# One chain for the rotation angles, and the index work of the first layer set behind later weight units

## The reference, cut to what matters

```
inv = ROPE_THETA ** (-arange(0, 64, 2) / 64)
ang = positions[..., None] * inv                    # 256 x 32
cos, sin = cos(ang), sin(ang)                       # tables of all rotations
for l in range(2):
    proj = rmsnorm(x, norm_mix[l]) @ w_in[l]        # 1024 -> 5956 columns
    aq, ak, av, iq, ik, iw, hq, hf, hi, hg, ga, gb = split(proj)
    aq = rope(rmsnorm(aq)); ak = rope(rmsnorm(ak))  # 8 heads of 64
    iq = rope(iq); ik = rope(ik)                    # 4 index heads, one key
    score = sum_h iw[h] * relu(iq[h] @ ik.T)        # 256 x 256, causal
    keep the 64 best keys of each query; softmax attention of q, k, v over them
    lb = cumsum(softmax(hgrn_lower_bound))[l] - ... # forget gate's lower bound
    ...                                             # recurrence, gates, output, SwiGLU
```

## Time and profile before

| | |
|---|---|
| median of 3 runs | 1150.14 us (1149.94 to 1151.73) |
| the profiled execution | 1151.75 us, span 1149.7 us |
| PE busy | 1113.0 us, 97% |
| DVE busy | 861.6 us, 75% |
| ACT busy | 622.6 us, 54% |
| `w_lo` on DVE (L1583) | 178 instructions, 401.3 us |
| `w_hi` on ACT (L1054) | 178 instructions, 336.3 us |
| mean DMA rate | 187 GB/s |

### The profile page before, as it was taken

The page is one execution under the profiler, slowest core; times in us unless marked ns, Lnnn a source line. Parts: engine busy times, 40 slices in busy tenths (PEclk is TensorE's granted clock), DMA queues, the critical chain, the costliest instruction groups (busy, mean ns, idle before and its releaser), DMA issues.

```text
span 1149.7 us, 20164 instructions
## 1 busy us (share of the span) xinstructions
PE 1113.0 (97%) x8452; PEld 1065.2 (93%) x8452; DVE 861.6 (75%) x1357; ACT 622.6 (54%) x780; POOL 0.2 (0%) x4
## 2 busy tenths in 40 slices
PE   5999999999999999999999999999999988999997
PEld 5899999999999998999999999999998868999997
DVE  7997766777988877986767788898699966545444
ACT  7677465554444356584664644344588576334333
POOL 0000000000000000000000000000000000000000
PEclk9999999999999999999999999999999998999999
DMA  9646444747879554564346568796555154555520
GB/s 345 210 147 186 145 147 144 254 153 261 278 249 318 164 169 149 156 199 157 122 135 227 193 224 280 245 316 209 160 148 176 43 185 147 184 184 183 184 74 37
DMA packets 176394, 215.14 MB, mean 187 GB/s; under 512 B 5808, under 2 KB 157744, under 8 KB 176304
## 3 DMA queue, kind: packets, MB, share of 16 engines
q1 hardware_dynamic: 175616, 213.20, 56.8%
q10 hardware_dynamic: 688, 0.66, 0.2%
HBM read 212.79 MB, written 1.06 MB: 186 GB/s over the span
## 4 chain that ended last, share of the span: by engine, by line
PE 76%; DVE 17%; ACT 5%; issue 2%; DMA 1%; DVEq 0%; ACTq 0%
PE stream L552 16%; PE stream L554 16%; PE stream L553 16%; DVE w_lo L1583 6%; PE steps L552 6%; PE steps L553 6%; PE steps L554 6%; ACT w_hi L1054 2%; PE stream L636 1%; PE stream L638 1%; PE stream L637 1%; DVE conv_acc L2166 1%; PE steps L966 1%; PE stream L804 1%; DVE conv_acc L2180 1%
## 5 line engine op out<-in xcount | busy, mean ns | idle before, releaser
L1583 DVE TENSOR_TENSOR w_lo<-raw,w_hi 128x2048 fp32r<-128x2048 f32 (+2 forms) x178 | 401.3, 2265 | 175.4 <-ACT w_hi L1054 174.4
L1054 ACT ACTIVATE w_hi<-raw 128x2048 fp32r<-128x2048 f32 (+2 forms) x178 | 336.3, 1893 | 285.3 <-PE stream L554 247.7
L552 PE MATMUL stream<-h_hi,w_hi 128*128 128x256 f32 x1592 | 455.3, 286 | 3.3 <-DVE w_lo L1583 3.0
L553 PE MATMUL stream<-h_lo,w_hi 128*128 128x256 f32 x1592 | 450.4, 283 | 0.0
L554 PE MATMUL stream<-h_hi,w_lo 128*128 128x256 f32 x1592 | 450.4, 283 | 0.0
L552 PEld LDWEIGHTS stream<-h_hi,w_hi 128*128 128x128 f32 x1592 | 305.2, 192 | 7.8 <-DVE w_lo L1583 5.1
L553 PEld LDWEIGHTS stream<-h_lo,w_hi 128*128 128x128 f32 x1592 | 305.4, 192 | 1.4 <-issue 1.0
L554 PEld LDWEIGHTS stream<-h_hi,w_lo 128*128 128x128 f32 x1592 | 305.3, 192 | 0.0
L552 PE MATMUL steps<-gu_hi,w_hi 128*128 128x256 f32 x352 | 99.9, 284 | 0.2 <-DVE gu_lo L1885 0.2
L553 PE MATMUL steps<-gu_lo,w_hi 128*128 128x256 f32 x352 | 99.6, 283 | 0.0
L554 PE MATMUL steps<-gu_hi,w_lo 128*128 128x256 f32 x352 | 99.6, 283 | 0.0
(11 more groups left out here) (367 smaller groups left out, 1620.0 us busy)
## 6 DMA issues: line engine op xcount, KB each, us to landing
raw<-in_w_ffn_in SPq DMA_DIRECT2D x66, 1024.0 KB, 5.7
raw<-in_w_in SPq DMA_DIRECT2D x54, 1024.0 KB, 5.4
raw<-in_w_ffn_out SPq DMA_DIRECT2D x33, 1024.0 KB, 5.1
ada_raw<-in_ada_w SPq DMA_DIRECT2D x24, 1024.0 KB, 6.4
raw<-in_w_out SPq DMA_DIRECT2D x8, 1024.0 KB, 5.1
raw<-in_w_proj_attn SPq DMA_DIRECT2D x8, 512.0 KB, 3.5
raw<-in_w_proj_hgrn SPq DMA_DIRECT2D x8, 512.0 KB, 4.5
raw<-in_w_o SPq DMA_DIRECT2D x4, 1024.0 KB, 4.9
```

Source lines behind the costliest of these rows:

```text
L552: pe.matmul(dst, w_h, x_h, start=start, stop=False, skip_group_check=True)
L553: pe.matmul(dst, w_h, x_l, start=False, stop=False, skip_group_check=True)
L1054: return act.activation(out_, in_, func, **kw)
L1583: tt(wl[m % SPL][:, 0:n], raw[m % RAW][:, 0:n], wh[m % SPL][:, 0:n].bitcast(F32), ALU.subtract)\
```

## The change

Three edits, all of them in the first layer (b = 0):

1. `setup_rope` runs one chain for sine and cosine together, on 128x128 numbers where both can share an instruction, and is cut in three by `yield`: DVE does the angles, turns and rounding, then the low part of unit 2, then the rest of the chain.
2. PE does unit 3 before the index transposes, and unit 4 before the index scores. To make up, one unit fewer stands behind the scores.
3. ACT does the copies `iqT` and `ikT`, and the exponential behind them, in the round j = 1 instead of j = 0.

```diff
@@ PE, mixer
-            stream(1)
+            stream(1 if b else 2)
             pe.wait_ge(*i_rot.at(b, 0))
             transposes([A[1]], iq, i_t, 2)
@@ PE, mixer, behind the index scores
-            stream(2)
+            stream(2 if b else 1)
             pe.wait_ge(*qk_rot.at(b, 0))
@@ ACT, mixer
                 if j:
                     unit_in()
                     wide_evac(q_tm)
-                else:
+                if j == (b == 0):
                     for i, (dst, src) in enumerate(((iqT.rearrange("p c t -> p (c t)"), A[1]), (ikT, A[2][:, 0:T]))):
                         act.wait_ge(*i_t.at(b, i))
                         f(dst, src, ACT.Copy).then_inc(*lane.mark(iT_set))
@@ DVE, mixer
-                setup_rope()
+                rope = setup_rope()
+                next(rope)
                 split(2)
+                next(rope)
                 setup_tables()
@@ DVE, setup_rope
-            ang = rope_w[:, 0]
+            ang, k, r = rope_w[:, 0], rope_w[:, 1:3], rope_w[:, 3:5]
             for t in range(NT):
                 ts_(ang[:, t, :], inv, posf[:, t:t + 1], None, ALU.mult).then_inc(*lane.step())
-            for i, (dst, turn, add) in enumerate(((sinT[:, :, 32:64], 0.0, 0.0), (cosT[:, :, 0:32], 0.25, math.pi / 2))):
-                k, r = rope_w[:, 1 + 2 * i], rope_w[:, 2 + 2 * i]
+            dve.wait_ge(*lane.last)
+            for i in range(2):
+                ts_(k[:, i], ang, 1 / two_pi, 0.25 * i, ALU.mult, ALU.add).then_inc(*lane.step())
+            dve.wait_ge(*lane.last)
+            ts_(k, k, magic, magic, ALU.add, ALU.subtract).then_inc(*lane.step())
+            yield
+            src = ang.unsqueeze(1).broadcast_to([P, 2, NT, 32])
+            for p_ in parts:
                 dve.wait_ge(*lane.last)
-                ts_(k, ang, 1 / two_pi, turn, ALU.mult, ALU.add).then_inc(*lane.step())
-                dve.wait_ge(*lane.last)
-                ts_(k, k, magic, magic, ALU.add, ALU.subtract).then_inc(*lane.step())
-                src = ang
-                for p_ in parts:
-                    dve.wait_ge(*lane.last)
-                    stt(r, k, -p_, src, ALU.mult, ALU.add).then_inc(*lane.step())
-                    src = r
-                dve.wait_ge(*lane.last)
-                ts_(r, r, add, math.pi * (1 - 1e-7), ALU.add, ALU.min).then_inc(*lane.step())
-                dve.wait_ge(*lane.last)
-                ins = ts_(dst, r, -math.pi * (1 - 1e-7), None, ALU.max)
-                ins.then_inc(*lane.mark(rope_arg)) if i else ins.then_inc(*lane.step())
+                stt(r, k, -p_, src, ALU.mult, ALU.add).then_inc(*lane.step())
+                src = r
+            dve.wait_ge(*lane.last)
+            for i in range(2):
+                ts_(r[:, i], r[:, i], i * math.pi / 2, math.pi * (1 - 1e-7), ALU.add, ALU.min).then_inc(*lane.step())
+            dve.wait_ge(*lane.last)
+            ts_(sinT[:, :, 32:64], r[:, 0], -math.pi * (1 - 1e-7), None, ALU.max).then_inc(*lane.step())
+            ts_(cosT[:, :, 0:32], r[:, 1], -math.pi * (1 - 1e-7), None, ALU.max).then_inc(*lane.mark(rope_arg))
+            yield
```

## The result

The changed kernel takes 1153.08 us in the median of 8 runs (1152.79 to 1154.84), the kernel before 1150.78 of 8 (1149.94 to 1151.75): ratio 1.0029, 95% interval 1.0020 to 1.0038. A second set of runs gave 1.0027 (1.0018 to 1.0036), with medians of 1153.29 and 1150.02. The change makes the kernel 0.3% slower. There the eight times of the kernel before fall into two groups of four, near 1150.0 and near 1151.7, and the median lies between them; those of the changed kernel lie near 1153.1 (six) and 1154.8 (two). Group against group the change costs 3.0 to 3.1 us, where the medians differ by 2.3. The profiled execution took 1154.76 us against 1151.75.

What follows compares the result with a forecast made beforehand. PE, busy 97%, was taken as the bound, paced by DVE at unit 10. DVE's stretch 3.9 us late (4.95 less 1.04), carried whole to the end, takes the median from 1150.14 to 1154.0; range 1152.5 to 1155.8.

Steps and rivals of the forecast that it cites:

- DVE's stall: DVE waits near 31.5 us for the lower bound's exponential, some 5.5 us, going on at 37.2 instead of 32.26.
- the stretch: DVE's work from unit 6's low part to unit 10's, 36.38 us: unchanged, 3.9 us late, carried whole to the end.
- some 4 us: Sign of being right: PE's idle time up to unit 10's low part is some 4 us more than before.
- Size of the stall's shift: DVE's stretch, and with it unit 10's start on PE, comes 3.9 us late (exponential 4.95 late, less 1.04).
- the time PE saves by unit 3: Unit 3 on PE ends 3.3 to 3.65 us earlier, taken as 3.5: unit 2 sooner, units 2 and 3 adjoining.
- The waits that vanish: Two DVE waits go in exchange for the stall: 0.96 us for unit 6's high part and 0.08 of overlap.
- Rope chain: DVE's wide subtractions take 0.25 to 0.37 us each; DVE comes to the tables 0.3 us earlier, at most 0.8.
- Rival 1: PE's new waits between 39 and 78 us bring a lower clock: about +1.5 if behind 77.5, total 1155.5; 13%.
- Rival 2: The exponential doesn't hold DVE: unit 10 comes 1.35 us sooner and caps the gain, 1148.8; 7%.
- Rivals 3 and 4: DVE's stretch shrinks: 1152.6 (5%) or 1146.7 (2%); table load drains 1.38 us: 1155.4 (5%, shared with later unit 2).

Runs made afterwards that it cites:

- e1: Changed kernel with the lower bound's exponential and its table load put back into ACT's round j = 0, ahead of unit 6's high part; 0.9982 against the kernel before.
- e4: Kernel before with only the lower bound's exponential moved on ACT behind the emptying of the queries (round j = 1); 1.0063 against the kernel before.
- e3: Kernel before with only the order on PE and ACT changed (transposes, scores, copies, exponential), rotation chain as before; 1.0055 against the kernel before.
- e8: Kernel before with the lower bound's eight DVE steps behind the exponential moved behind the low part of unit 12; 0.9997 against the kernel before.
- e5: e1 with the cast of the masks moved into DVE's wait for the cosines; 0.9981 against the kernel before.
- e6: e5 with the lower bound's eight DVE steps also moved behind the low part of unit 12; 0.9967 against the kernel before.
- e9: e6 with ACT computing the squares of the queries ahead of the copies iqT and ikT; 0.9958 against the kernel before, 1145.61 us median.
- e2: Kernel before with only the rotation chain changed (one chain, cut around the low part of unit 2); 1.0003 against the kernel before.
- e10: The changed kernel run again, unaltered, for more runs and a second trace; 1.0027 against the kernel before.

## Why the prediction was right

The mechanism was right in all its steps: the exponential behind unit 3 on ACT, DVE's stall (5.60 us for some 5.5), the stretch carried whole to unit 10, PE's waits at units 5, 9, 10 and at the query and key transposes, and nothing given back behind them (3.42 us late at the second layer, 3.43 at unit 10). The time forecast was 1154.0 and the median is 1153.08. Of these 0.9 us about half is the size named next; the rest can't be told from the groups of times. PE's idle time from 20 to 79 us grew by 3.1 us (59 - 52.84 against 59 - 55.95), where "some 4 us" was the sign. e1 and e4 show the cause from both sides: with only the exponential put back the loss becomes a gain, and with only the exponential moved the loss is there without the rest.

- **Size of the stall's shift.** +3.9 was forecast at unit 10, +3.4 to +3.5 came; +3.0 to +3.1 of it shows in the times, group against group. The step that was off is the time PE saves by unit 3. I took 3.5 from the bounds 3.3 to 3.65, and it was 3.93 (ACT's high part of unit 6 at 31.39 instead of 35.32): unit 2 starts 0.13 us behind the start of the transposes L899, not behind their end, so it gained 2.03 and not 1.73, and 1.9 came from joining units 2 and 3. The earlier PE is, the less the loss. So the exponential came 4.50 us late and not 4.95. The waits that vanish (1.04) were right: 4.50 - (40.74 - 37.26) = 1.02.
- **Rope chain.** The four wide subtractions took 1.27 us together, 0.32 each, between the bounds of 0.25 and 0.37 and not at the upper one; the cosines were at 21.26 on DVE, 0.8 sooner than before and not 0.3. It changed nothing, as the stall came behind it.
- **Rival 1, lower clock.** In both traces of the changed kernel the granted clock was 1.00 from 20 to 79 us, so the new waits brought no lower clock there. In e3 they may have: behind a wait of 1.95 us that ends at 42.87 it has a stretch at 0.50 (first row below), and unit 10 is as late as DVE makes it, so such a stretch is hidden there, as the rival said. In the changed kernel's trace one falls at 889 us (second row), where the kernel before had none. It needs no new waits, since e8, whose unit 10 came as before, has one there too (0.54 from 885.5 to 889.0). It cost 0.2 us (the shift on PE is 3.47 us ahead of it and 3.67 us behind it), because most of it filled a wait that PE has there in the kernel before (third row).

```profile
43.70:47.10 3.40, 3.40 (x10) 2.62 (x9) 3.40 (x4) 0.52 (x2) 0.00 (x0) 0.50 0.95 283
889.10:892.50 3.40, 3.40 (x19) 3.40 (x18) 3.37 (x18) 1.29 (x2) 0.00 (x0) 0.50 0.34 101
893.73 0.66 PE L778 MATMUL steps<-consts,y_of_heads 128*128 128x128 f32 x4 [0.86 <-DVE y_of_heads L1786]
```

- **Rival 2** (the exponential doesn't hold DVE) is e1: 1.35 us sooner was its forecast, and e1 is 1.9 us sooner at unit 10 and in its median (1148.21 against 1150.15). The 0.5 us more match the chain's gain on DVE, 0.8 us and not the 0.3 in the rival's sum. That unit 10 caps the gain was right: PE waits 1.32 us there.
- **Rivals 3 and 4.** DVE's stretch didn't shrink in any kernel where it had a stall: 34.04 us in the changed one, e1, e3 and e4, against 34.10. The drain of the Trainium skill ("ScalarE: Activation LUTs", What ACT_TABLE_LOAD costs) didn't show around this load either: 1.29 us from its start to the exponential, in ACT's rows above.

## What to carry to other kernels

When a step is moved on an in-order engine, look at each instruction that travels with it, however small, and at who waits for it: here an exponential of 0.21 us rode along with two copies and held the engine that set the pace. Ask of every wait removed which engine is late next: shortening DVE's list was worth nothing while PE's unit 3 started DVE's stretch (e8), and each saving moved unit 10 once PE was early (e5, e6, e9). Savings on two engines that pace each other in turn belong together; alone, one can look worthless, as e8 did.

## What the runs showed of the hardware

The times of one kernel fall into groups about 1.5 to 2 us apart: the kernel before gave 1147.7 to 1148.0, 1150.0 to 1150.3 and 1151.4 to 1152.0 in 28 of its 30 runs of one set. The groups go with the mean granted clock of each run: it was 0.995 or 0.996 in the four runs of the first, 0.994 in the twelve of the second and 0.992 in the twelve of the third. The traces give a reason for such steps. The same work, from the norm sum of the second layer to the wait at its unit 10, at a granted clock of 0.97 in the kernel before (one stretch at the lower level) and of 1.00 in e1:

```profile
424.37:480.87 56.50, 55.89 (x325) 49.00 (x325) 48.41 (x86) 32.67 (x40) 0.00 (x0) 0.97 0.49 150
```

```profile
422.55:477.51 54.96, 54.35 (x324) 47.46 (x324) 48.41 (x86) 32.68 (x40) 0.00 (x0) 1.00 0.51 154
```

56.50 against 54.96: 1.54 us for one such stretch. In both kernels PE had waited about 1.9 us just before (1.88 and 1.90), so the length of the wait doesn't decide; the same kernel has the stretch in one run and not in another (the changed kernel: there in its first trace, not in e10's). The Trainium skill, "TensorE: Matmul & The Clock Gate", What's actually happening, says that the activity is looked at in windows that run free of the kernel, which fits that. I hadn't expected it to explain the spread of the runs, nor that a saving can be hidden by it, as in e2. That the slower groups have the lower mean clock shows in these 30 runs; that it comes in stretches like these shows in the 12 traces only.
